# Expert feed-forward on one core: the gate product in 512-column matmuls, and the next expert's first product in two halves around the second product

## The reference

```python
# router: sigmoid scores, grouped top-k, normalized gates; each token goes to two experts
h = silu(tok @ w1[e]) * (tok @ w3[e])      # w1, w3: 1024 x 512
y[e] = h @ w2[e]                           # w2: 512 x 1024
out = sum over the token's experts of gate * y[e]
```

## Time and profile before

| | us |
|---|---|
| median of 3 runs | 1727.56 (1726.68 to 1731.23) |
| the profiled execution, its own time | 1723.7 |
| its span in the profile | 1721.9 |
| TensorE busy in the span | 1661.8 (97%) |
| VectorE busy | 1154.4 (67%) |
| ScalarE busy | 1008.9 (59%) |
| experts of the first layer, about | 310 to 637 |
| experts of the second layer, about | 970 to 1280 |

### The profile page before, as it was taken

One profiled execution on the slowest core, in us unless ns is written; L12 is line 12 of the kernel. 1 busy time (PEld: TensorE's weight loads), 2 busy tenths in 40 slices (PEclk: granted clock), 3 DMA queues, 4 the chain that ended last, 5 costly groups with the idle time before them and its releaser, 6 DMA issues.

```text
span 1721.9 us, 29951 instructions
## 1 busy us (share of the span) xinstructions
PE 1661.8 (97%) x12176; PEld 1426.4 (83%) x12176; DVE 1154.4 (67%) x1594; ACT 1008.9 (59%) x1335; POOL 64.9 (4%) x66
## 2 busy tenths in 40 slices
PE   6999999999999999999999899999999999999998
PEld 4787676889888868888989688888878998897688
DVE  5432874799989985343366798998975687544564
ACT  4322763588888876224354588888865573454561
POOL 0000000000000010000000000000000000100100
PEclk9999999999999999999999999999999999999999
DMA  8745215899999964223574599999974554274612
GB/s 345 216 131 235 111 49 207 316 405 404 404 409 407 390 256 150 87 95 147 196 286 186 189 387 411 400 408 406 395 275 152 191 191 154 74 232 160 165 57 74
DMA packets 52556, 419.79 MB, mean 244 GB/s; under 512 B 16980, under 2 KB 18132, under 8 KB 30048
## 3 DMA queue, kind: packets, MB, share of 16 engines
q1 hardware_dynamic: 26416, 364.56, 53.4%
q0 software_dynamic: 8304, 31.64, 6.1%
q10 hardware_dynamic: 17728, 22.02, 3.9%
HBM read 398.23 MB, written 19.97 MB: 243 GB/s over the span
## 4 chain that ended last, share of the span: by engine, by line
PE 84%; DVE 7%; DMA 4%; ACT 2%; issue 2%; POOL 0%; SPq 0%; ACTq 0%; DVEq 0%; POOLq 0%
PE ps L767 50%; PE ps L913 17%; PE ps L728 4%; DMA ring<-w_all 3%; PE ps L751 2%; PE ps L922 1%; DVE w_lo L2343 1%; PE ps L1158 1%; PE ps L1169 1%; PE ps L1184 1%; PE ps L929 1%; DMA y_d<-arena 1%; PE ps L774 1%; PE ps L807 1%; PE ps L1373 1%
## 5 line engine op out<-in xcount | busy, mean ns | idle before, releaser
L2343 DVE TENSOR_TENSOR w_lo<-ring,w_hi 128x1024 fp32r<-128x1024 f32 x384 | 452.2, 1220 | 49.3 <-ACT w_hi L1673 48.0
L1673 ACT ACTIVATE w_hi<-ring 128x1024 fp32r<-128x1024 f32 x384 | 397.8, 1058 | 101.4 <-PE ps L913 60.0
L767 PE MATMUL ps<-XT_lo,arena_r 128*128 128x256 f32 (+1 forms) x1712 | 384.8, 300 | 2.6 <-DVE arena L3022 1.3
L767 PEld LDWEIGHTS ps<-XT_lo,arena_r 128*128 128x128 f32 x1712 | 281.3, 190 | 17.9 <-issue 3.5
L913 PE MATMUL ps<-w_hi,x_hi 128*128 128x256 f32 (+1 forms) x768 | 250.0, 325 | 5.7 <-issue 4.4
L913 PE MATMUL ps<-w_lo,x_hi 128*128 128x256 f32 (+1 forms) x768 | 245.4, 320 | 0.0
L913 PE MATMUL ps<-w_hi,x_lo 128*128 128x256 f32 (+1 forms) x768 | 245.4, 320 | 0.0
L767 PE MATMUL ps<-arena_r 128*128 128x512 f32 (+1 forms) x656 | 230.6, 359 | 6.6 <-DVE arena_r L2526 2.5
L767 PE MATMUL ps<-XT_lo,ring_r 128*128 128x256 f32 x640 | 180.7, 282 | 0.0
L2200 DVE TENSOR_TENSOR ring_r<-ring,arena_r 128x1024 fp32r<-128x1024 f32 x96 | 114.0, 1222 | 98.2 <-ACT arena_r L1575 98.1
L913 PEld LDWEIGHTS ps<-w_hi,x_hi 128*128 128x128 f32 x768 | 146.5, 191 | 23.5 <-issue 7.3
(11 more groups left out here) (384 smaller groups left out, 2635.8 us busy)
## 6 DMA issues: line engine op xcount, KB each, us to landing
ring<-w_all SPq DMA_DIRECT2D x172, 2048.0 KB, 9.6
y_d<-arena ACTq DMA_DIRECT2D x30, 512.0 KB, 10.0
arena<-toep_d POOLq DMA_DIRECT2D x16, 384.0 KB, 11.7
arena<-rpb ACTq DMA_DIRECT2D x16, 192.0 KB, 3.8
xtok_d<-arena ACTq DMA_DIRECT2D x6, 512.0 KB, 3.0
hT<-h SPq DMA_DIRECT2D x2, 1024.0 KB, 6.9
arena<-cb_d POOLq DMA_DIRECT2D x1, 1536.0 KB, 11.8
arena<-cc_d POOLq DMA_DIRECT2D x1, 959.0 KB, 9.5
```

What stands on the lines that cost most here:

```text
L767: last = nc.tensor.matmul(out, a, b, start=(first and i == 0), stop=(final and i == 2))
L1673: nc.scalar.activation(w_hi[:, q], slot(b, "p (q c) -> p q c", q=4)[:, q], ACT.Copy).then_inc(hi_rdy, 1)
L2343: nc.vector.tensor_tensor(w_lo[:, q], slot(base + n, "p (q c) -> p q c", q=4)[:, q], as_f32(w_hi[:, q]), ALU.subtract).then_inc(*split_sig ...
```

## The change

For experts 1 to 14 of both layers:

- w3 is stored by rows like w1, and u3 is made in four quarters of six matmuls with 512 columns into bank 3. The gate product is one VectorE instruction over 512 columns, and so is ACT's high part of the hidden rows; the low part stays in halves.
- `turn_rows` of the next expert moves up, behind the first quarter of u3.
- While the gate product and the splits of the hidden rows run, TensorE makes the first half of the next expert's u1, with the four transposes of the hidden rows between its two quarters; then y; then the second half of that u1. The blocks are repacked for it: after w3[e] comes a block with the first half of w1[e+1] and the first half of w2[e], then one with the second half of w2[e] and the second half of w1[e+1].
- ACT and DVE follow in that order; ACT stores y before the splits of the second and third quarter of the next w3 instead of after the splits of the next w1. The small VectorE instructions of experts 1 and 14 move.

Experts 0 and 15 keep their halves of u3. At a layer's start the first expert's rows are copied bank by bank: the first bank's copy waits for the fourth of eight chains only, DVE does two comparisons ahead of the first weight split, and makes `x_lo` before the list of rows. The dense branch follows the new block order.

```diff
@@ TensorE, routed
+                def second_matrix(e, quarters):
+                    for k, (e2, n2, q) in enumerate(quarters):
+                        if k == 2:
+                            pe.wait_ge(f_he, e * 2 + (2 * c + 2))
+                        quarter_wait(e2, n2, q)
...
+                def turn(e, j, half_e):
+                    pe.wait_ge(f_h, e * 2 + 2 * c)
+                    for q in range(4):
+                        quarter(e, j, 1, q, ps[:, 3, :], (2 * q, 2 * q + 1), 512, q == 0, q == 3, (f_u3, 2) if q == 3 else None)
+                        if q == 0:
+                            turn_rows(e + 1, 1 - j, half_e + j)
+                    rows_copied(e + 1)
+                    pe.wait_ge(f_s, e + (c + 1))
+                    for q in range(4):
+                        if q == 2:
+                            pe.wait_ge(f_he, e * 2 + (2 * c + 1))
+                            pe.wait_ge(f_ya, e + c)
+                            second_matrix(e, ((e, 2, 2), (e, 2, 3), (e + 1, 0, 0), (e + 1, 0, 1)))
+                        quarter(*((e, 1 - j, 2) if q < 2 else (e + 1, 1 - j, 0)), q, ps[:, 2, :], (2 * q, 2 * q + 1), 512,
+                                q == 0, q == 3, (f_u1, 1) if q == 3 else None)
+                        if q == 0:
+                            pe.wait_ge(f_h, e * 2 + (2 * c + 2))
+                            pe.wait_ge(f_he, e * 2 + 2 * c)
+                            turn_hidden(j, 0)
+                            turn_hidden(j, 1)
@@ ScalarE, routed
+                def turn(e, j, half_e):
+                    split(e, 1, (3,))
+                    gate(e, j)
+                    split(e, 2, (0,))
+                    copy_rows(e + 1, 1 - j)
+                    split(e, 2, range(1, 4))
+                    act.wait_ge(f_ht, e * 2 + (2 * c + 2))
+                    nc.scalar.activation(ehT_hi, ps[:, 4, :].rearrange("p (k s) -> p k s", k=4), ACT.Copy).then_inc(f_hh, 2)
+                    split(e + 1, 0, range(4))
+                    split(e + 1, 1, (0,))
+                    rows_of_y(e, j, half_e)
+                    split(e + 1, 1, (1, 2))
...
+                split(0, 0, (0, 1))
+                for b in range(2):
+                    act.wait_ge(*((f_x, c + 1) if b else (pos_mm, 2 * layer + 2)))
+                    nc.scalar.activation(x_hi[:, 0, 4 * b:4 * b + 4], ps[:, b, :].rearrange("p (k s) -> p k s", k=4),
+                                         ACT.Copy).then_inc(f_xa, 1)
@@ VectorE, routed
+                def turn(e, j):
+                    split(e, 1, (3,))
+                    split(e, 2, (0,))
+                    copy_rows(e + 1, 1 - j)
+                    split(e, 2, (1,))
+                    dve.wait_ge(f_u3, e * 2 + (2 * c + 2))
+                    dve.wait_ge(f_s, e + (c + 1))
+                    nc.vector.tensor_tensor(eh[:, j], es[:, j], ps[:, 3, :], ALU.mult).then_inc(f_h, 2)
+                    split(e, 2, (2,))
+                    hidden_lo(e, 0)
+                    split(e, 2, (3,))
+                    hidden_lo(e, 1)
+                    split(e + 1, 0, (0, 1))
+                    if isinstance(e, int) and e == 1:
+                        two_rows()
+                    split(e + 1, 0, (2, 3))
+                    if isinstance(e, int) and e == 1:
+                        rows_taken()
+                    split(e + 1, 1, (0, 1))
+                    if isinstance(e, int) and e > 1:
+                        gates_taken()
+                    split(e + 1, 1, (2,))
@@ host: order of the blocks
+        out = [w1[0], w3[0], w2[0], w1[1]]
+        for e in range(1, EXPERTS - 1):
+            out += [w3k[e], np.concatenate([w1[e + 1][:, :half], w2[e][:, :half]], 1),
+                    np.concatenate([w2[e][:, half:], w1[e + 1][:, half:]], 1)]
+        return np.stack(out + [w3[EXPERTS - 1], w2[EXPERTS - 1]])
```

More of the change, by code:

```diff
@@ L930, in turn_hidden, with rows_copied, first_matrix, turn_halved @@
                     last.then_inc(f_ht, 1)
-                def turn(e, j, first, last_e, half_e):
-                    some = not (first and j == 0)
-                    pe.wait_ge(f_xa, e + (c + 1))
+                def rows_copied(e):
+                    pe.wait_ge(f_xa, e + (cx + 1))
                     pe.wait_ge(f_xd, e + (c + 1))
[L936 to L942, removed]
-                    for q in range(4):
-                        quarter(e, j, 0, q, ps[:, 2, :], (2 * q, 2 * q + 1), 512, q == 0, q == 3, f_u1 if q == 3 else None)
-                    if some:
+                def first_matrix(e, j):
+                    for q in range(4):
+                        quarter(e, j, 0, q, ps[:, 2, :], (2 * q, 2 * q + 1), 512, q == 0, q == 3, (f_u1, 1) if q == 3 else None)
+                def second_matrix(e, quarters):
[3 more added lines that the diff above has]
+                        quarter_wait(e2, n2, q)
+                        for n in range(2):
+                            cols = slice(n * 512, (n + 1) * 512)
+                            last = three_terms(ps[:, 5 + n, :], ehT_hi[:, k], ehT_lo[:, k], w_hi[:, q, cols], w_lo[:, q, cols],
+                                               k == 0, k == 3)
+                            if k == 3:
+                                last.then_inc(f_d, 1)
+                        if k < 3:
+                            last.then_inc(split_used, 1)
+                def turn_halved(e, j, last_e):
+                    if last_e:
                         pe.wait_ge(f_h, e * 2 + 2 * c)
@@ L968, in turn @@
                     turn_hidden(j, 1)
-                    if some:
+                    if last_e:
                         pe.wait_ge(f_ya, e + c)
[L972 to L983, removed]
+                    second_matrix(e, [(e, 2, q) for q in range(4)])
+                def turn(e, j, half_e):
[18 more added lines that the diff above has]
+                            turn_hidden(j, 1)
                 list_rows(1, range(1, 2))
@@ L987, in routed @@
                     warm(3, 3)
[L988 to L989 removed]
+                rows_copied(0)
+                first_matrix(0, 0)
+                turn_halved(0, 0, False)
+                rows_copied(1)
+                pe.wait_ge(f_s, c + 1)
+                pe.wait_ge(ix_rdy, 2 * layer + 2)
+                if layer == 0:
+                    mod_cols_of(15, 7, after=9)
+                first_matrix(1, 1)
+                turn(1, 1, 0)
                 with pe.Fori(1, EXPERTS // 2 - 1) as i:
                     for j in range(2):
[L992 to L994 removed]
+                        turn(i * 2 + j, j, i)
+                turn(EXPERTS - 2, 0, EXPERTS // 2 - 1)
+                turn_halved(EXPERTS - 1, 1, True)
                 def turn_tile(t, m):
@@ L2371, in turn, with turn_last @@
+                def turn_last(e, j):
+                    split(e, 1, (3,))
                     gate_half(e, j, 0)
-                    if first and j == 1:
-                        two_rows()
                     split(e, 2, (0, 1))
@@ L2449, in dense @@
                 if layer == 0:
+                    dve.wait_ge(mt_mm, 16)
                     mods_out(13, 7, 72)
```

201 lines of the change are left out of this document (119 added, 82 removed).

## The result

The changed kernel took 1739.41 us (median of 4 runs, 1736.2 to 1741.82) against 1727.12 us before: 1.0059 times as long, 95% interval 1.0040 to 1.0077, some 10 us slower (the medians lie 12.3 apart). The profiled execution has a span of 1739.9 us, 18.0 more than before; the difference is larger there because the profiled execution before, 1723.7, was a quick one for its kernel, and the one after, 1741.82, the longest of four.

The account below looks back on a forecast made before the run. TensorE was taken to pace the loop, with DMA share also 1.00. 26 periods at 17.87 instead of 18.09 us give -5.7, the rest +0.55, total -5.2: 1722.4 us; range 1713 to 1735, likeliest 1719 to 1724.

Parts of the forecast that it names:

- the store of y and the ring: Loop: slots held 7.8, 8.3 and 6.7 us; hold plus load, 8.3 plus 9.3 for the mixed block, fits 17.87.
- the lower price: Loop: load time of 8.7 us with the ring to itself, against 10.0 at the median; 9.3 taken for the mixed block.
- Rival 2: Loop: mixed block's slot comes back late, TensorE waits in every expert; period 18.3, +6.0 us, 1733.6 us; chance 0.17.
- The path to the gate: Loop, from y's last product to the hidden transposes: TensorE waits between nothing and 0.15 us for the single gate.
- No slack: Loop, hidden rows' splits: they end at about F + 12.3, TensorE at F + 12.4 (F: y's last product ends); no second wait.
- TensorE's own work: Loop: u3 in 512 columns saves 0.32 us per expert; with the pauses kept, the period is 17.77 us.
- The start: First expert of a layer: first matrix at 317.45, hidden transposes at 330.7; gain 2.45 us, in the second layer 0.2.
- The cost of the moved half of u1: Order of the experts: half of the next u1 stands ahead of expert 14's y, +2.72 us per layer.
- The tail: End of the experts' stage: y's copy comes 0.2 us after the product instead of 1.16; 0.95 us sooner per layer.

Follow-up runs that it names:

- y's copy late: Changed kernel with ScalarE's copy and store of y moved from between w3's first two quarters to behind the next block's second quarter: 1724.5 us, ratio 0.9984.
- the two kernels that took 1739 us: The changed kernel, 1739.41 us, and the kernel with y's copy late whose w3 slot is loaded again one split later, 1739.13 us.

## Why the prediction was wrong

I forecast 1722.4 us and a period of 17.87; it was 1739.4 and 18.7, the mean of both layers.

The step that failed stands in the paragraph on the store of y and the ring: "The mixed block's load is issued long after the previous one, so I take it nearer the lower price, 9.3, which fits 17.87." The holds themselves were right: 7.8, 8.3 and 6.7 forecast, 7.4, 8.4 and 6.7 measured. The loads were not. I priced one load, by a row of the old rhythm, and looked at one block. All three loads changed, to 11.3, 9.9 and 11.7, and the block that was used as it landed in ten experts of eleven was w3's, of which I had only written down the hold: 7.4 + 11.3 is 18.7. Nor was the lower price that of a load alone, as I wrote: the next load was issued 3.05 us after it, at 316.16. The trace of before had part of what was needed. There the blocks lay ready 2.4, 0.5 and 1.3 us, and a hold of 8.3 beside the load of 10.1 that w2's block took there makes 18.4, not 17.87. What it did not have is that w3's load would grow to 11.3.

Rival 2 was the right mechanism, slots that come back late, with the wrong block and size. Its own point of decision, a load of more than 9.8 us for the mixed block, was just passed (9.9), but that block still lay ready 0.45 us in the mean and w3's 0.1; it gave +0.21 us per expert and it was +0.65. It took the load as fixed, while the loads grew longer when the slots came free at other times.

The path to the gate was sized nearly right. I put the wait at nothing to 0.15; without late blocks it is 0.16. What I missed is that TensorE waits for x_lo ahead of the gate. "No slack", as I wrote it, was the real warning: a block 0.76 us late cost nothing before, since the gates of the halves had room, and now it reaches TensorE.

TensorE's own work came out nearly: w3's products 0.227 apart, and a floor of 17.90, against 17.77 with no wait. So 0.18 of the 0.32 us that the long matmuls save reaches the period; by the account of the earlier trace rows the rest went into longer pauses where the kind of work changes.

The start was right on its own rows: 317.34 for 317.45, 330.47 for 330.7. That the start alone gave 2.8 us for 2.65 may be partly luck, since its trace shows only 1.4 of it at the end of the first layer. The cost of the moved half of u1 is about right: from expert 14's Silu to the end of its y it is 2.0 us longer in both layers, where 2.72 less the 0.32 of u3 was forecast. The tail was half right: the copy does follow the product at once, but in the first layer the rest took 22.9 us and not 21.64, so the gain of 0.95 was lost there; in the second it took 19.5 and not 19.91, and the gain came. The store of expert 14's y went the same way, 1.45 us longer and 1.0 shorter; no run tested what sets its time.

In sum, outside the 24 periods counted above the span grew by 2.5 us, and in them by 15.5. The forecast had +0.55 for the first, with 26 periods, and -5.7 for the second. The 2.5 is the difference of two single executions, and the four timed ones before lie up to 5.6 us apart, so nothing hangs on it.

What stays open in part is why the loads got longer. Most of it is time behind the load ahead (2.1 of 2.8 us, above), with issues at uneven distances. That is no general rule: with y's copy late w3's load took 11.4 us with only 4.2 of it behind the one ahead. And in the two kernels that took 1739 us the DMA moved less (389 and 388 GB/s from 350 to 585 us) than in the kernel before (405) or with y's copy late (403), at a share of 0.98 and 0.99, so they did not ask for more than it had given. Whether loads in each other's way or transfers of y and rows beside them slow it down was not shown; no run changed the transfers alone.

## What to carry to other kernels

When a change moves work between a block's first and last use, add up hold plus load for every slot of the ring and compare it with the period, and read from the trace how long each block lies ready before its first split: that is all the slack there is. Do it for the worst load and not the mean: in the table above one block's load took 9.05 to 11.8 us at the mean, in kernels whose slots come free at different times. A copy and store of 1.6 us on an engine that is only 84% busy is not free if it stands between the first and the last use of a buffer that is waited for. And a saving on the bounding engine comes through only if the waits that had slack before still have it afterwards.

## What the runs showed of the hardware

A ring of three slots at a DMA share of 1.00 turned out to be steep: beside y's copy late, to load one slot again a split later (hold 8.0 us for 6.4) cost 0.77 us per expert in the first layer, to load it again only when x_lo is made, one instruction further (8.6), 1.36, though in both kernels another block lay ready 2 us. And a DMA share near 1.00 does not tell the rate: 389 GB/s was moved at 0.98, 405 at 1.00.

With half the load TensorE's period was the same to 0.01 us in the kernel before (18.08), so a full DMA beside it did not slow its matmuls.
